# Retrieval layer of a hybrid decoder: splits of the tiles that run ahead moved to GpSimd, one-hot rows moved to VectorE, SyncE's order changed

## The chip, the cores and the metric

One core of one Trainium2 chip runs the whole program. The metric is the device time of one execution in microseconds (us); of several executions the median is given.

## The reference

The program is one inference step of a two-layer decoder for 512 prompt tokens and 32 sample tokens. Each layer has a mixer (attention with a gated recurrence in layer 0, a convolution module in layer 1) and then a retrieval over 128 x 128 experts, which is what the change touches:

```python
q = (xb @ w_q).reshape(blk, PEER_HEADS, 2, PEER_DKH)
sc = jnp.einsum('nhpd,hpkd->nhpk', q, sub_keys)
sv, si = lax.top_k(sc, PEER_TOPK)
cand = sv[:, :, 0, :, None] + sv[:, :, 1, None, :]
cidx = si[:, :, 0, :, None] * N_KEYS + si[:, :, 1, None, :]
fv, fi = lax.top_k(cand, PEER_TOPK)
eidx = jnp.take_along_axis(cidx, fi, axis=-1)
gate = jax.nn.softmax(fv, axis=-1)
act = gelu(einsum('nd,nhed->nhe', xb, u_tab[eidx]))
y = einsum('nhe,nhed->nd', gate * act, v_tab[eidx])
```

Every token has 8 heads with 16 chosen experts each. An expert number is a pair of keys (first key, second key), each from 0 to 127.

## The kernel before, in words

For 384 of the tokens (three blocks of 128, `DENSE`) the kernel gathers nothing. It multiplies all tokens with all experts in tiles of 128 experts: 128 tiles of the table U ("units") and 128 of the table V ("values") in each layer, with a gate matrix between them that is zero where a token did not choose an expert. The other two blocks (`LONE`) gather their rows by indirect DMAs on GpSimd.

A tile's way: SyncE loads it (512 KB) into one of four `raw` buffers. ScalarE copies it to the ring in a rounded format (`hi`, L1005). The difference of the two, the low part, is the **split** (`low` on VectorE, L1572; `lo` on GpSimd, L1902, which is used for the tiles of the projections only). Then TensorE takes it: `units` (L850) makes 24 matmuls of 384 columns, `values` (L862) 18 of 512. Matmuls of a tile wait for `lo_ready`, and for units also for the Gelu (L1091) of the tile two before, since there are two PSUM halves.

While the gate matrix is not there, 48 units tiles run ahead (`AHEAD`); their Gelu results go through three buffers `ga` (`ASLOT`) to DRAM by SyncE (`write_units`) and come back later. In this time the ring has four slots only, so `hi` of tile i + 3 waits for the matmuls of tile i - 1. The stage goes thus, in each layer:

- **Front**: 26 tiles (`FRONT`). VectorE makes the choices of three token blocks (`select`, 15 parts, two LONE blocks and the first DENSE one) with the splits between the parts (`SEL_QUANTA`).
- **Gates with tiles**: 32 groups of eight tokens (16 for each of blocks 0 and 1), a tile after each second group (`MID` = 16 tiles). For a group VectorE and ScalarE make two sets of eight one-hot rows: `oh1`, first key times gate weight, eight `tensor_scalar` on VectorE (L1560); `oh2`, second key, three on VectorE (L1556) and five on ScalarE (`Abs` into `dist`, L1052, then one `Relu`, L1057). TensorE multiplies them (`gate_group`, L833), ScalarE stages the result (`stage_group`, L1123 and L1129). Between the groups VectorE makes the next block's choice, one part after each group, and after each second group the split of one tile.
- **Gates alone**: the last 16 groups, with no tile between them, two one-hots of eight on ScalarE.
- **Six tiles** (42 to 47), then two more units tiles and the first tile of values.

After every eighth group SyncE writes the staged 4 MB to DRAM in two DMAs (`write_gates`); the staging buffer is single, so ScalarE's first copy of the next eight waits for them. TensorE may be two groups ahead of ScalarE's copies and VectorE two ahead of TensorE. `choice` (L819) transposes a block's choices on TensorE; ScalarE copies them (`slT`, L1137) and the block's one-hots can begin.

Every engine works through its own list in the order in which it is written; SyncE's list (`experts`, L450) goes by tiles: at step i it loads tile i + 7 (after the split of tile i + 3, which had the same raw buffer), then writes the unit of tile i - 2. GpSimd's list has the gathers (`gather_rows`) next; they wait until all groups are staged.

Of the kernel before, what the change touches and what calls it, by code (L numbers as in the profile page):

```python
# [21 lines left out]
F32 = mybir.dt.float32  # L22
F32R = mybir.dt.float32r
U32 = mybir.dt.uint32
ALU = mybir.AluOpType
# [3 lines left out]
P = 128  # L29
# [18 lines left out]
ACT_OH_BUSY, ACT_OH_FREE = 5, 2  # L48
# [21 lines left out]
AHEAD, FRONT, MID = 48, 26, 16  # L70
# [31 lines left out]
def ready_by(i):  # L102
# [4 lines left out]
SEL_QUANTA = [(0, (0,)), (0, (1, 2, 3, 4, 5)), (0, (6, 7, 8, 9, 10, 11, 12, 13, 14))] + [  # L107
    (i, parts) for i in (1, 2) for parts in ((0,), (1, 2), (3, 4, 5), (6, 7), (8,), (9, 10), (11,), (12, 13), (14,))]
EXP_AFTER = {[m for m, (s, parts) in enumerate(SEL_QUANTA) if s == i and 4 in parts][0]: i for i in range(3)}

# [78 lines left out]
def build(nc, xT, stream, utab, vtab, params, consts, mconsts, reset, keysT, kcacheT, vcache, kvcache_n, state_h, convT,  # L189
          yT, kwin_p, vwin_p, hs_p, cb_p, kwin_s, vwin_s, hs_s, cb_s):  # L190
    ctx = ExitStack()
    with ctx:
# [84 lines left out]
        with ExitStack() as z:  # L277
            with ExitStack() as zz:
                hf_peer = sb("hf_peer", [P, KC, NT], F32, zz)
            with ExitStack() as zz:  # L280
                oh2 = sb("oh2", [P, 2, 8, P], F32, zz)
                oh1 = sb("oh1", [P, 2, 8, P], F32, zz)
            sb("ohpad", [P, KC * NT], F32, z)
            with ExitStack() as zz:
                keys = sb("keys", [P, 16, P], F32, zz)
                qh = sb("qh", [P, 2, NT], F32, zz)
                sc2 = sb("sc2", [P, 4, P], F32, zz)
            with ExitStack() as zz:
                ga = sb("ga", [P, ASLOT, ND], F32, zz)
                pick = sb("pick", [P, 3, 16, NCAND], F32, zz)  # L290
            sb("keypad", [P, 16 * P + 2 * NT + 5 * P], F32, z)
            sv = sb("sv", [P, NTILE, 16, 16], F32, z)
            si = sb("si", [P, NTILE, 16, 16], U32, z)
            sif = sb("sif", [P, 16, 16], F32, z)
            cand = sb("cand", [P, 8, NCAND], F32, z)
            cand2 = sb("cand2", [P, 8, NCAND], F32, z)
            cidx = sb("cidx", [P, 8, NCAND], F32, z)
            fv = sb("fv", [P, 8, 16], F32, z)
            fi = sb("fi", [P, 8, 16], U32, z)
            pos = sb("pos", [P, 8, 16], F32, z)  # L300
            eidx = sb("eidx", [P, 8, 16], F32, z)
            r16 = sb("r16", [P, 8, 16], F32, z)
            r8 = sb("r8", [P, 2, 8], F32, z)
            sel = sb("sel", [P, 3, 8, 16], F32, z)
            slT = sb("slT", [P, 2, 3, P], F32, z)
            dist = sb("dist", [P, max(ACT_OH_BUSY, ACT_OH_FREE), P], F32, z)
# [102 lines left out]
        def _(sp):  # L409
# [40 lines left out]
            def experts(l):  # L450
                for i in range(7):
                    load_expert(l, i)
                for i in range(N_EXP):
# [4 lines left out]
                    if i >= AHEAD - 2 and tile_at(i + 4)[1]:  # L458
                        load_gate(l, V_SEQ[tile_at(i + 4)[2]])
                    if i + 7 < N_EXP:  # L460
                        load_expert(l, i + 7)
                    if 2 <= i < AHEAD + 2:
                        write_units(l, i - 2)
                    h, r = divmod(i - FRONT - 3, 4)
                    if r == 0 and 0 <= h < 3:
                        write_gates(l, h)
                    if i == FRONT + MID - 1:
                        for h in range(3, 6):
                            write_gates(l, h)
# [65 lines left out]
        s_oh = sem("dve_onehots_ready")  # L535
        s_oha = sem("act_onehots_ready")
# [53 lines left out]
        def _(pe):  # L590
# [246 lines left out]
            def experts(l):  # L837
# [33 lines left out]
                for m in range(MID):  # L871
                    gate_group(l, 2 * m)
                    gate_group(l, 2 * m + 1)
                    if m % 8 == 7:
                        choice(l, m // 8 + 1)
                    units(FRONT + m)
                for g in range(2 * MID, ND // 8):
                    gate_group(l, g)
                for i in range(FRONT + MID, AHEAD):
                    units(i)  # L880
# [115 lines left out]
        def _(act):  # L996
# [48 lines left out]
            def onehots(l, n, q):  # L1045

                e = (ND // 8) * l + n * 16 + q
                k = ACT_OH_BUSY if n + 1 < NDB else ACT_OH_FREE
                if e:
                    act.wait_ge(s_oha, e)  # L1050
                for i in range(k):
                    ch.done(A.activation(dist[:, i, :], iota, ACT.Abs, scale=-1.0,  # L1052
                                         bias=slT[:, n % 2, 1, 8 * q + i:8 * q + i + 1]))
                ch.sync()
                if n * 16 + q >= 2:
                    act.wait_ge(s_gm, e - 1)
                A.activation(oh2[:, e % 2, 0:k, :], dist[:, 0:k, :], ACT.Relu, scale=-1.0,  # L1057
                             bias=ones[:, 0:1]).then_inc(s_oha, 1)

# [21 lines left out]
            def experts(l):  # L1081
# [19 lines left out]
                def tile_step(i):  # L1101
# [5 lines left out]
                    if i < FRONT and i - 1 in EXP_AFTER:  # L1107
                        select_exp(l, EXP_AFTER[i - 1])
# [26 lines left out]
                for n in DENSE:  # L1135
# [3 lines left out]
                    act.wait_ge(s_slT, NDB * l + n + 1)  # L1139
                    onehots(l, n, 0)  # L1140
                    for q in range(16):
                        if q + 1 < 16:
                            onehots(l, n, q + 1)
# [3 lines left out]
                        if q % 2 and n + 1 < NDB:  # L1147
                            tile_step(FRONT + 8 * n + q // 2)
                for i in range(FRONT + MID, N_EXP):
# [230 lines left out]
        def _(dve):  # L1380
# [164 lines left out]
            def onehots(l, n, q):  # L1545
# [6 lines left out]
                k = ACT_OH_BUSY if n + 1 < NDB else ACT_OH_FREE  # L1552
                if n * 16 + q >= 2:
                    dve.wait_ge(s_gm, e - 1)
                for j in range(k, 8):
                    ch.done(V.tensor_scalar(oh2[:, e % 2, j, :], iota, slT[:, n % 2, 1, 8 * q + j:8 * q + j + 1],  # L1556
                                            None, ALU.is_equal))
# [9 lines left out]
            def experts(l):  # L1567
# [47 lines left out]
                def tile_step(i):  # L1615
                    for j in range(ready_by(i - 1) if i else 3, ready_by(i)):
                        low(t0 + j)

                dve.wait_ge(s_lo, t0 + 3)
                for i in range(FRONT):  # L1620
                    if i < len(SEL_QUANTA):
                        s, parts = SEL_QUANTA[i]
                        for part in parts:
                            select(l, s, part)
                    tile_step(i)
                for n in DENSE:
                    for q in range(16):
                        onehots(l, n, q)
                        if n + 1 < NDB:
                            if q >= 1:  # L1630
                                select(l, 3 + n, q - 1)
                            if q % 2:
                                tile_step(FRONT + 8 * n + q // 2)
                n_row = 0
                for i in range(FRONT + MID, N_EXP):
                    tile_step(i)
# [262 lines left out]
        def _(pool):  # L1899
# [9 lines left out]

            def gather_rows(l):  # L1910
# [40 lines left out]
            lo_run(T_WQ[0], T_WQ[0] + N_WQ + 3)  # L1951
            gather_rows(0)
# [10 lines left out]
            lo_run(T_WQ[1], T_WQ[1] + N_WQ + 3)  # L1963
            gather_rows(1)
# [118 lines left out]
```

## Time and profile before

| | us |
|---|---|
| median of 3 executions | 3833.21 |
| lowest, highest | 3825.51, 3833.39 |
| the profiled execution | 3821.67 |
| its span, first to last instruction | 3819.9 |
| TensorE busy | 3301.6 (86%) |
| VectorE busy | 2786.7 (73%) |
| ScalarE busy | 1460.5 (38%) |
| GpSimd busy | 1190.3 (31%) |

All durations below come from the profiled execution, whose 3821.67 us are 1.77 us more than its span. The stage of the change comes twice: at 637.6 to 1128.3 us (layer 0) and at 2460.6 to 2953.6 us (layer 1). A row of the profile reads: line of the code, engine, operation, tile written<-tiles read, shapes, count, busy time, mean time of one in ns, idle time before it and what ended it. PE is TensorE, DVE VectorE, ACT ScalarE, POOL GpSimd, SP SyncE. A row of the timeline has start and length in us; several instructions in a row of one line are merged ("x8"), and their starts lie closer than their lengths, since one instruction's end overlaps the next one's start.

### The profile page before, as it was taken

What the parts mean: (1) busy time and instruction counts of PE and PEld (TensorE: products, weight loads), DVE (VectorE), ACT (ScalarE), POOL (GpSimd) and SP (SyncE); (2) the same over time, 40 slices, a digit from 0 to 9 for tenths busy, and PEclk for the clock granted to TensorE, in tenths of its full rate; (3) what the DMA queues carried; (4) which work ended last, traced back from release to release, by engine and by line L of the source; (5) the groups of instructions that cost most, each with busy time, mean ns of one, the idle gap of its engine ahead of it and who ended that gap; (6) DMA issues with size and microseconds to landing.
All of it is one profiled execution on the core that took longest, in us unless ns stands there. A gap on an engine that the chain in (4) does not pass through costs nothing. (4 is left out here: it accounts for less than half of the span.)

```text
span 3819.9 us, 50346 instructions
## 1 busy us (share of the span) xinstructions
PE 3301.6 (86%) x18573; PEld 3004.1 (79%) x18573; DVE 2786.7 (73%) x6082; ACT 1460.5 (38%) x2215; POOL 1190.3 (31%) x766
## 2 busy tenths in 40 slices
PE   6877899956679999999978879996667999999998
PEld 5767788955578888888867658986656888888887
DVE  4426457866658888888866964796665888888887
ACT  3433222466643333333323222236655333333332
POOL 2210321000025555555542112100001555555554
PEclk9988699988889999999998989998878999999999
DMA  3110312523269999999961141252235999999997
GB/s 116 47 48 1 96 63 77 167 90 112 97 250 381 363 361 363 366 361 361 361 234 61 39 54 52 67 167 98 90 126 205 380 365 364 369 359 363 360 364 264
DMA packets 424997, 807.91 MB, mean 212 GB/s; under 512 B 233953, under 2 KB 259105, under 8 KB 421281
## 3 DMA queue, kind: packets, MB, share of 16 engines
q1 hardware_dynamic: 318960, 454.23, 35.7%
q0 software_dynamic: 94560, 344.45, 24.3%
q10 hardware_dynamic: 11232, 6.01, 1.2%
q8 instruction: 148, 2.42, 0.3%
q14 instruction: 97, 0.79, 0.1%
HBM read 729.52 MB, written 76.08 MB: 211 GB/s over the span
## 5 line engine op out<-in xcount | busy, mean ns | idle before, releaser
L850 PE MATMUL bank<-hh,ring 128*128 128x384 f32 x4096 | 1096.2, 341 | 45.9 <-ACT ga L1091 36.7
L1572 DVE TENSOR_TENSOR ring<-raw,ring 128x1024 fp32r<-128x1024 f32 x506 | 618.3, 1223 | 458.7 <-ACT ring L1005 458.2
L1921 POOL DMA_INDIRECT rows<-in_utab,gidx x320 | 452.4, 1414 | 1335.9 <-ACT stage L1129 891.0
L862 PE MATMUL bank<-ring,wh 128*128 128x512 f32 x3072 | 828.3, 391 | 0.0
L850 PEld LDWEIGHTS bank<-hh,ring 128*128 128x128 f32 x4096 | 750.8, 190 | 58.5 <-issue 41.2
L1005 ACT ACTIVATE ring<-raw 128x1024 fp32r<-128x1024 f32 x598 | 622.1, 1053 | 193.9 <-PE bank L850 87.1
L850 PE MATMUL bank<-hl,ring 128*128 128x384 f32 x2048 | 691.0, 337 | 0.0
L862 PEld LDWEIGHTS bank<-ring,wh 128*128 128x128 f32 x3072 | 574.4, 188 | 111.3 <-issue 0.2
L1921 POOL DMA_INDIRECT rows<-in_vtab,gidx x320 | 491.1, 1535 | 368.4 <-DVE acc L1612 316.0
L611 PE MATMUL bank<-hh,ring 128*128 128x272 f32 x2752 | 493.8, 299 | 74.8 <-DVE hl L1397 43.5
L1091 ACT ACTIVATE ga<-bank 128x384 f32<-128x384 f32 x256 | 125.4, 490 | 1100.3 <-PE bank L850 997.3
L611 PEld LDWEIGHTS bank<-hh,ring 128*128 128x128 f32 x2752 | 408.9, 196 | 88.6 <-issue 51.6
L833 PE MATMUL bank<-oh 128*128 128x128 f32 x1536 | 258.8, 340 | 248.1 <-DVE oh L1560 214.7
L862 PE MATMUL bank<-ring,wl 128*128 128x512 f32 x1536 | 473.1, 389 | 0.0
L833 PEld LDWEIGHTS bank<-oh 128*128 128x128 f32 x1536 | 240.6, 247 | 269.7 <-DVE oh L1560 235.7
L1902 POOL TENSOR_TENSOR ring<-raw,ring 128x1024 fp32r<-128x1024 f32 x92 | 223.6, 2438 | 677.0 <-ACT ring L1005 674.4
L1612 DVE SCALAR_TENSOR_TENSOR acc<-rows,wv,acc 128x1024 f32<-128x1024 f32 x316 | 404.5, 1280 | 12.3 <-DVE acc L1612 0.5
L850 PEld LDWEIGHTS bank<-hl,ring 128*128 128x128 f32 x2048 | 389.5, 190 | 6.1
L1604 DVE CUSTOM_DVE_ANT_0 rows<-rows,htok 128x1024 f32<-128x1024 f32 x320 | 381.8, 1219 | 0.7 <-DMA rows<-in_utab,gidx 0.7
L862 PEld LDWEIGHTS bank<-ring,wl 128*128 128x128 f32 x1536 | 288.3, 188 | 64.1
L611 PE MATMUL bank<-hl,ring 128*128 128x272 f32 x1376 | 293.1, 295 | 0.0
L611 PEld LDWEIGHTS bank<-hl,ring 128*128 128x128 f32 x1376 | 226.1, 196 | 0.0
(299 smaller groups left out, 3166.6 us busy)
## 6 DMA issues: line engine op xcount, KB each, us to landing
raw<-in_stream SPq DMA_DIRECT2D x342, 512.0 KB, 4.4
raw<-in_vtab SPq DMA_DIRECT2D x256, 512.0 KB, 7.7
gate_matrix<-stage SPq DMA_DIRECT2D x24, 2048.0 KB, 10.2
gt<-gate_matrix SPq DMA_DIRECT2D x256, 192.0 KB, 9.4
units_ahead<-ga SPq DMA_DIRECT2D x96, 192.0 KB, 4.1
gv<-units_ahead SPq DMA_DIRECT2D x96, 192.0 KB, 8.8
rows<-in_utab,gidx POOLq DMA_INDIRECT x320, 7.9
rows<-in_vtab,gidx POOLq DMA_INDIRECT x320, 8.0
```

Of the source, the lines that this page charges most:

```text
L611: m = T.matmul(PA[t % 2][:, a, 0:HALF], w[:, ring_slot(t), k * P:(k + 1) * P], h[:, k, a * HALF:(a + 1) * HALF], start=(k == 0 and i == 0) ...
L833: m = T.matmul(PA[e % 2][:, i // 4, (i % 4) * P:(i % 4 + 1) * P], oh2[:, e % 2, i, :], oh1[:, e % 2, i, :], start=True, stop=True)
L850: m = T.matmul(PB[1][:, (e + 1) % 2, 0:ND], w[:, ring_slot(t), k * P:(k + 1) * P], h[:, k, 0:ND], start=(k == 0 and i == 0), stop=(k == KC ...
L862: m = T.matmul(psum[c][:, a, :], w[:, v_n % WSLOT, c * P:(c + 1) * P], v[:, ring_slot(t), 512 * a:512 * a + 512], start=(v_n == 0 and i == ...
L1005: A.activation(ring_hi[:, ring_slot(t), :], raw[b][:], ACT.Copy).then_inc(s_hi, 1)
L1091: A.activation(ga[:, e % ASLOT, :], PB[1][:, (e + 1) % 2, 0:ND], ACT.Gelu).then_inc(s_ga, 1)
L1572: V.tensor_tensor(ring_lo[:, ring_slot(t), :], raw[raw_buffer(t)][:], ring_hi[:, ring_slot(t), :].bitcast(F32), ALU.subtract).then_inc(s_l ...
L1604: V.tensor_tensor_reduce(out=rows[:, slot, :], in0=rows[:, slot, :], in1=htok[b][:, :], scale=1.0, scalar=0.0, op0=ALU.mult, op1=ALU.add, ...
L1612: V.scalar_tensor_tensor(out=acc[b][:, :], in0=rows[:, slot, :], scalar=wv[b][:, j:j + 1], in1=acc[b][:, :], op0=ALU.mult, op1=ALU.add).th ...
L1902: nc.gpsimd.tensor_tensor(ring_lo[:, slot, :], raw[buf][:], ring_hi[:, slot, :].bitcast(F32), ALU.subtract).then_inc(s_lo, 1)
L1921: nc.gpsimd.indirect_dma_start(out=rows[:, g % ROW_SLOTS, :], out_offset=None, in_=vtab if is_v else utab, in_offset=bass.IndirectOffsetOn ...
```

## The change

GpSimd makes the splits of tiles 3 to 47 in a list of its own (`ahead`), before the gathers. VectorE makes all of `oh2` with one `tensor_tensor` over 8 x 128 elements a group, and ScalarE makes no one-hots. VectorE makes the three choices of the front without splits between them. 24 tiles run in the front; in the gates, tiles come after groups 1, 3, 5 (one each) and 7 (two) of each eight for the first 32 groups, two come after group 39, and the last two after group 47. ScalarE's exponentials of the three choices (`select_exp`) come at tile steps 3, 8 and 19. SyncE writes unit i - 1 before it loads tile i + 7, and each `write_gates` stands at the step of the tiles that follow its eighth group.

```diff
-AHEAD, FRONT, MID = 48, 26, 16
+AHEAD, FRONT = 48, 24
...
+TILES_AFTER = [0] * (ND // 8)
+for _g in range(ND // 8):
+    if _g < 32:
+        TILES_AFTER[_g] = {1: 1, 3: 1, 5: 1, 7: 2}.get(_g % 8, 0)
+TILES_AFTER[39] = 2
+TILES_BEFORE = [FRONT + sum(TILES_AFTER[:_g]) for _g in range(ND // 8)]
+EXP_BEFORE = {3: 0, 8: 1, 19: 2}
...
+                    if 1 <= i <= AHEAD:
+                        write_units(l, i - 1)
                     if i + 7 < N_EXP:
                         load_expert(l, i + 7)
-                    if 2 <= i < AHEAD + 2:
-                        write_units(l, i - 2)
-                    h, r = divmod(i - FRONT - 3, 4)
-                    if r == 0 and 0 <= h < 3:
-                        write_gates(l, h)
-                    if i == FRONT + MID - 1:
-                        for h in range(3, 6):
+                    for h in range(ND // 64):
+                        if i == TILES_BEFORE[8 * h + 7] - 1:
                             write_gates(l, h)
...
-                for m in range(MID):
-                    gate_group(l, 2 * m)
-                    gate_group(l, 2 * m + 1)
-                    if m % 8 == 7:
-                        choice(l, m // 8 + 1)
-                    units(FRONT + m)
-                for g in range(2 * MID, ND // 8):
+                i = FRONT
+                for g in range(ND // 8):
                     gate_group(l, g)
-                for i in range(FRONT + MID, AHEAD):
+                    for m in range(TILES_AFTER[g]):
+                        units(i)
+                        i += 1
+                        if g % 16 == 15 and m == 0:
+                            choice(l, g // 16 + 1)
+                for i in range(i, AHEAD):
                     units(i)
...
-                    onehots(l, n, 0)
                     for q in range(16):
-                        if q + 1 < 16:
-                            onehots(l, n, q + 1)
                         stage_group(n, q)
                         if q == 6 and n + 1 < NDB:
                             select_exp(l, 3 + n)
-                        if q % 2 and n + 1 < NDB:
-                            tile_step(FRONT + 8 * n + q // 2)
-                for i in range(FRONT + MID, N_EXP):
+                        for m in range(TILES_AFTER[16 * n + q]):
+                            tile_step(TILES_BEFORE[16 * n + q] + m)
+                for i in range(TILES_BEFORE[-1], N_EXP):
                     tile_step(i)
...
-                for j in range(k, 8):
-                    ch.done(V.tensor_scalar(oh2[:, e % 2, j, :], iota, slT[:, n % 2, 1, 8 * q + j:8 * q + j + 1],
-                                            None, ALU.is_equal))
+                V.tensor_tensor(oh2[:, e % 2, :, :], iota.unsqueeze(1).to_broadcast([P, 8, P]),
+                                slT[:, n % 2, 1, 8 * q:8 * q + 8].unsqueeze(2).to_broadcast([P, 8, P]),
+                                ALU.is_equal).then_inc(s_oha, 1)
...
-                dve.wait_ge(s_lo, t0 + 3)
-                for i in range(FRONT):
-                    if i < len(SEL_QUANTA):
-                        s, parts = SEL_QUANTA[i]
-                        for part in parts:
-                            select(l, s, part)
-                    tile_step(i)
+                for i in range(3):
+                    for part in range(NPART):
+                        select(l, i, part)
                 for n in DENSE:
                     for q in range(16):
                         onehots(l, n, q)
-                        if n + 1 < NDB:
-                            if q >= 1:
-                                select(l, 3 + n, q - 1)
-                            if q % 2:
-                                tile_step(FRONT + 8 * n + q // 2)
+                        if n + 1 < NDB and q >= 1:
+                            select(l, 3 + n, q - 1)
+                dve.wait_ge(s_lo, t0 + AHEAD)
                 n_row = 0
-                for i in range(FRONT + MID, N_EXP):
-                    tile_step(i)
+                for i in range(AHEAD - 3, N_EXP):
+                    for j in range(ready_by(i - 1), ready_by(i)):
+                        low(t0 + j)
...
+            def ahead(l):
+
+                def tile_step(i):
+                    for j in range(ready_by(i - 1) if i else 3, min(AHEAD, ready_by(i))):
+                        lo(T_EXP[l] + j, ring_slot(T_EXP[l] + j), raw_buffer(T_EXP[l] + j))
+
+                for i in range(FRONT):
+                    tile_step(i)
+                for g in range(ND // 8):
+                    for m in range(TILES_AFTER[g]):
+                        tile_step(TILES_BEFORE[g] + m)
+
...
             lo_run(T_WQ[0], T_WQ[0] + N_WQ + 3)
+            ahead(0)
             gather_rows(0)
```

## Rows read from the trace of the kernel before

**Rows 1.** Windows by stage, layer 0: length, busy time by engine, clock, DMA share, GB/s.
```profile
637.60:761.10 123.50, 114.57 (x627) 111.12 (x627) 111.62 (x327) 51.24 (x71) 4.62 (x2) 0.97 0.54 159
761.10:1016.80 255.70, 157.20 (x902) 148.78 (x902) 166.61 (x575) 159.24 (x267) 0.00 (x0) 0.83 0.28 96
1016.80:1083.30 66.50, 37.51 (x257) 35.27 (x258) 48.67 (x210) 42.12 (x59) 0.00 (x0) 0.85 0.31 131
1083.30:1128.30 45.00, 35.02 (x193) 34.73 (x192) 14.77 (x18) 14.79 (x19) 8.96 (x7) 0.89 0.83 289
```

**Rows 2.** Waits, 761.1 to 1083.3 us: total us, times, longest.
```profile
PE bank L833 <- DVE oh L1560: 110.1, 39, 13.4
DVE ring L1572 <- ACT ring L1005: 88.0, 16, 13.1
DVE oh L1556 <- PE bank L833: 15.8, 3, 8.4
```

**Rows 3.** Timeline of VectorE in the gates with tiles.
```profile
784.21 1.23 DVE L1572 TENSOR_TENSOR ring<-raw,ring 128x1024 fp32r<-128x1024 f32 x1 [3.75 <-ACT ring L1005]
785.35 0.67 DVE L1556 TENSOR_SCALAR oh<-con,slT 128x128 f32<-128x128 f32 x3
785.94 2.14 DVE L1560 TENSOR_SCALAR oh<-con,slT 128x128 f32<-128x128 f32 x8
```

**Rows 4.** VectorE by line, 644.95 to 741.2 us (the front's three choices).
```profile
L1572 DVE TENSOR_TENSOR ring<-raw,ring 128x1024 fp32r<-128x1024 f32 x21 | 25.6, 1217 | 0.0
L1516 DVE TENSOR_TENSOR pick<-pick,cidx 128x2400 f32<-128x2400 f32 (+1 forms) x7 | 16.1, 2301 | 0.2
L1507 DVE TENSOR_TENSOR pick<-pos,con 128x2400 f32<-128x2400 f32 (+1 forms) x7 | 16.1, 2295 | 0.0
```

**Rows 5.** Waits of the front, 637.6 to 761.1 us.
```profile
ACT ga L1091 <- DMA units_ahead<-ga: 36.2, 16, 5.5
```

**Rows 6.** GpSimd and VectorE by line, 2050 to 2160 us (convolution, layer 1).
```profile
L1902 POOL TENSOR_TENSOR ring<-raw,ring 128x1024 fp32r<-128x1024 f32 x12 | 32.3, 2713 | 69.6 <-ACT ring L1005 69.6
...
L1873 DVE SCALAR_TENSOR_TENSOR cv<-up,par,cv 128x512 f32<-128x512 f32 x87 | 69.9, 803 | 0.0
L1873 DVE SCALAR_TENSOR_TENSOR cv<-us,par,cv 128x32 f32<-128x32 f32 x86 | 35.6, 414 | 0.0
```

**Rows 7.** Timeline of VectorE there, beside splits by GpSimd.
```profile
2058.02 2.37 DVE L1871 TENSOR_SCALAR cv<-us,par 128x32 f32<-128x32 f32 x1
...
2060.76 0.29 DVE L1871 TENSOR_SCALAR cv<-us,par 128x32 f32<-128x32 f32 x1
...
2093.82 0.24 DVE L1873 SCALAR_TENSOR_TENSOR cv<-us,par,cv 128x32 f32<-128x32 f32 x1
2093.98 0.75 DVE L1873 SCALAR_TENSOR_TENSOR cv<-up,par,cv 128x512 f32<-128x512 f32 x1
2094.64 2.41 DVE L1873 SCALAR_TENSOR_TENSOR cv<-us,par,cv 128x32 f32<-128x32 f32 x1
```

**Rows 8.** GpSimd and VectorE by line, 2340 to 2422 us (retrieval, layer 1).
```profile
L1902 POOL TENSOR_TENSOR ring<-raw,ring 128x1024 fp32r<-128x1024 f32 x12 | 28.8, 2400 | 91.7 <-ACT ring L1005 91.7
...
L1454 DVE FIND_INDEX8 si<-sv,sc 128x8 uint32<-128x128 f32 x40 | 10.7, 285 | 0.0
```

**Rows 9.** The chain that ended last, layer 1's gates alone: start, length.
```profile
2841.03 12.96 DMA gate_matrix<-stage
2873.05 2.07 PE bank L833 x16
2875.14 1.95 ACT stage L1129
2877.47 10.80 DMA gate_matrix<-stage
2909.38 4.18 PE bank L850 x24
```

**Rows 10.** DMA issues (the page): KB each, median us to landing.
```profile
gt<-gate_matrix SPq DMA_DIRECT2D x256, 192.0 KB, 9.4
```

More of the change, by code:

```diff
@@ L47 @@
 DENSE, LONE = (0, 1, 2), (4, 3)
-ACT_OH_BUSY, ACT_OH_FREE = 5, 2
 NPART = 15
@@ L104, in ready_by @@
     return min(N_EXP, i + (4 if i < AHEAD + 4 else 5))
-SEL_QUANTA = [(0, (0,)), (0, (1, 2, 3, 4, 5)), (0, (6, 7, 8, 9, 10, 11, 12, 13, 14))] + [
-    (i, parts) for i in (1, 2) for parts in ((0,), (1, 2), (3, 4, 5), (6, 7), (8,), (9, 10), (11,), (12, 13), (14,))]
-EXP_AFTER = {[m for m, (s, parts) in enumerate(SEL_QUANTA) if s == i and 4 in parts][0]: i for i in range(3)}
+TILES_AFTER = [0] * (ND // 8)
[5 more added lines that the diff above has]
+EXP_BEFORE = {3: 0, 8: 1, 19: 2}
 ROW_SLOTS = 5
@@ L305, in build @@
             slT = sb("slT", [P, 2, 3, P], F32, z)
-            dist = sb("dist", [P, max(ACT_OH_BUSY, ACT_OH_FREE), P], F32, z)
         with ExitStack() as z:
@@ L534, in build @@
         s_slT = sem("selection_T_ready")
-        s_oh = sem("dve_onehots_ready")
-        s_oha = sem("act_onehots_ready")
+        s_oh = sem("key1_onehots_ready")
+        s_oha = sem("key2_onehots_ready")
         s_ht = sem("lone_tokens_transposed")
@@ L1043, in attn_out @@
                     .then_inc(s_oe, 1)
[L1045 to L1058, printed above, removed]
             def retrieval(l):
@@ L1106, in tile_step @@
                         hi(t0 + j)
-                    if i < FRONT and i - 1 in EXP_AFTER:
-                        select_exp(l, EXP_AFTER[i - 1])
+                    if i in EXP_BEFORE:
+                        select_exp(l, EXP_BEFORE[i])
                     if i and not tile_at(i - 1)[1]:
@@ L1138, in experts @@
                                  ACT.Copy).then_inc(s_slT, 1)
-                    act.wait_ge(s_slT, NDB * l + n + 1)
-                    onehots(l, n, 0)
                     for q in range(16):
-                        if q + 1 < 16:
-                            onehots(l, n, q + 1)
                         stage_group(n, q)
@@ L1551, in onehots @@
                         dve.wait_ge(s_ht, 2 * (l + 1))
-                k = ACT_OH_BUSY if n + 1 < NDB else ACT_OH_FREE
                 if n * 16 + q >= 2:
                     dve.wait_ge(s_gm, e - 1)
-                for j in range(k, 8):
-                    ch.done(V.tensor_scalar(oh2[:, e % 2, j, :], iota, slT[:, n % 2, 1, 8 * q + j:8 * q + j + 1],
-                                            None, ALU.is_equal))
+                V.tensor_tensor(oh2[:, e % 2, :, :], iota.unsqueeze(1).to_broadcast([P, 8, P]),
+                                slT[:, n % 2, 1, 8 * q:8 * q + 8].unsqueeze(2).to_broadcast([P, 8, P]),
+                                ALU.is_equal).then_inc(s_oha, 1)
                 for j in range(8):
@@ L1613, in row @@
                                                in1=acc[b][:, :], op0=ALU.mult, op1=ALU.add).then_inc(s_rd, 1)
-                def tile_step(i):
-                    for j in range(ready_by(i - 1) if i else 3, ready_by(i)):
-                        low(t0 + j)
-                dve.wait_ge(s_lo, t0 + 3)
-                for i in range(FRONT):
-                    if i < len(SEL_QUANTA):
-                        s, parts = SEL_QUANTA[i]
-                        for part in parts:
-                            select(l, s, part)
-                    tile_step(i)
+                for i in range(3):
+                    for part in range(NPART):
+                        select(l, i, part)
                 for n in DENSE:
@@ L1963, in _ @@
             lo_run(T_WQ[1], T_WQ[1] + N_WQ + 3)
+            ahead(1)
             gather_rows(1)
```

## The prediction, made before the changed kernel was run

> **What bounds the kernel now.** I read the windows by stage first. Before its values begin (at 1128.3 us in layer 0), a layer spends 490.7 us on tiles that run ahead and on gates; layer 1 spends 493.0 (from 2460.6 to 2953.6). There TensorE is busy for 157.2 of 255.7 us in the gates with tiles and for 37.5 of 66.5 in the gates alone, at a granted clock of 0.83 to 0.85 of 2.4 GHz [rows 1]. So the waits come next. TensorE waits 110.1 us for VectorE's one-hots, but VectorE is not full either (166.6 of 255.7): it waits 88.0 us for ScalarE's copies before the 16 splits [rows 1, 2]. The timeline shows the loop: the split (it had waited 3.75 us) stands ahead of the next one-hots [rows 3]; it waits for a copy, the copy for a ring slot, the slot for a tile on TensorE, and that tile stands behind the groups that wait for one-hots. In the front VectorE has no idle time while it makes the three choices, from 645 to 741 us, with 21 splits among them [rows 4]. So VectorE sets the front's pace and a closed loop through VectorE, TensorE and ScalarE that of the gates. The chain of waits adds the DMA of the staged gates, 10.8 to 13 us for four MB [rows 9].
>
> **What the change costs and gives, per layer.** *A split on GpSimd* takes 2.40 us [rows 8], less than the 4.18 us of a tile (24 matmuls, [rows 9]), and its result is needed three tiles later; so GpSimd keeps up. Its price falls on VectorE. In the convolution twelve splits by GpSimd ran beside VectorE's two-input and scalar operations: one of 32 columns took 2.41 us where its like took 0.24, a `tensor_scalar` 2.37 for 0.29 [rows 7]. Twelve splits made the 86 short ones mean 414 ns and the 87 long ones 803 instead of 240 and 750 [rows 6, 7], that is 15.0 + 4.6 us, and two `tensor_scalar` some 4 more: 24 us, **2.0 us of VectorE a split** when VectorE does nothing else. `FIND_INDEX8`, with one input, keeps its 285 ns beside GpSimd [rows 8]. No row shows a reduction or the choices beside a split. The ends are 0 and 2.4 us a split (GpSimd's whole length); I weigh the 2.0 by the share of VectorE's time in operations like those that were held, and take a reduction as free, since it has one input like `FIND_INDEX8`.
>
> *Front.* 96.25 us hold 21 splits of 1.14 us (784.21 to 785.35 in [rows 3]), so the choices alone are 72 us. The two large two-input groups are 32.2 of them [rows 4]; with the small two-input and scalar ones I estimate 41, a share of 0.57, so 1.2 us a split. While they last GpSimd makes some 23 (one a tile): 645 + 72 + 27 = 744 us. TensorE would end its 23rd tile at 637.6 + 6 (the first one, at the lower clock) + 22 x 4.18 = 736, so it waits for `choice` until 744. Transpose and copy take two more: first one-hots at 746, against 758.4 (0.59 + 2.1 us of one-hots before the first group at 761.1, [rows 1, 3]). **Gain 12.** SyncE's new order takes away the 36.2 us that ScalarE waited for units written late [rows 5]: the write no longer stands behind a load that waits for a split. I cost it at nothing, since the choices cover it; were they shorter, TensorE's 736 would be the next to be late. The load now stands behind the Gelu, but that follows the copy, and the split that the load waits for anyway ends later.
>
> *Gates with tiles.* VectorE's work is 166.6 - 16 x 1.23 = 147 us. One `oh2` of 8 x 128 replaces three that take 0.59 us (785.35 to 785.94): 1024 elements took 1.14 from start to start [rows 3], and repeated operands cost no more by the row, 2295 ns for the 2400 and 1600 elements of L1507 [rows 4]: +0.55 x 32 = 18. Twenty splits at 1.7 (one-hots and two-input parts are 138 of 165 us, 0.84 of the time, by 2.0) are 34. Two hand-overs to the next block, in which `slT` waits behind ScalarE's second tile step, are 5 each. 147 + 18 + 34 + 10 = 209 us against 255.7. **Gain 46.** TensorE's work in it, 32 groups of 2.05 and 20 tiles of 4.18, is 149 us at the full clock, so VectorE is the bound. ScalarE loses its share of the one-hots; it was not last, so that is nothing by itself. The four tiles more than before are TensorE time inside VectorE's. After each eighth group two tiles (8.3) and two groups cover the 13 us write. SyncE waits for that eighth group with one unit write and the loads behind it; seven tiles are loaded by then, so nobody waits.
>
> *Gates alone.* A group costs VectorE 1.14 + 2.05 = 3.2 us as before (six `tensor_scalar` and eight). First group to last: seven groups 22.4, two splits 4; then group 40's copy waits for the write: 2.07 + 1.95 + 11 to 13 after the one-hots of group 39, 1 for the copy, 2.07 for group 42, four sets of one-hots: 32; last group 2. Sum 60.5 against 66.5. **Gain 6.**
>
> *Tail.* Before, 45.0 us with 35 of TensorE work (eight tiles). After: four tiles, 17 us; but the first value's gates come later: copy 2, write 13, `gt` 9.4 [rows 10], product and its two parts 3: 27.5. **Gain 17.** GpSimd's gathers stand behind its splits, but they wait for the last group in any case.
>
> Sum 81 a layer. VectorE's waits for TensorE were 15.8 us [rows 2]; under the new rhythm they lie between nothing and that again, and since two octet ends made most of them I take 3. That is 78 a layer, 156 for both. The profiled execution took 3821.7 us: **3666 us**. It lies 11.5 below the median shown, so a median may come out some 10 above.
>
> **Rivals.** *A, the lock is cheap:* splits fall into operations with one input, or GpSimd waits and VectorE doesn't. Then the front is TensorE's (one-hots at 738, gain 20) and the gates cost 180 instead of 209: 37 more a layer, **3592**. For it: the splits start at the same point of each round. Against it: a one-hot set is 3.2 us of nothing but two-input and scalar operations.
>
> *B, more is lost than the sum has:* full 2.4 a split in the front (choices end at 772, a loss of 16 instead of a gain of 12), 2.4 in the gates (-14), TensorE at the lower clock after its pauses so that VectorE waits 15 instead of 3. Gain 24 to 36 a layer (the second without the lower clock), **3750 to 3774**. The clock of 0.83 [rows 1] speaks for some of this; VectorE's slack of two groups against it.
>
> *C, slower: the splits only change hands.* If VectorE's 88.0 us for copies come back as a wait for TensorE's groups (the loop closes through the one-hots' buffers instead of the ring), then 43 splits cost 2.0 instead of 1.17, which is 36 a layer, and `oh2` 18 more; the tail gives 17 back: 37 lost a layer, **3896**. It decides where a round of two groups and a tile takes TensorE longer than VectorE's 12.6 us; by the rows it takes 8.3, and 16.5 if all of it ran at 1.2 GHz. The Trainium skill's page Perfetto Trace Analysis, section Optimizing Scalar/DVE Operations, warns that moving work between VectorE and GpSimd might not help, as they share a port; by that rule this case would be the likely one. The trace agrees on the sharing (2.41 us for 0.24, [rows 7]), but there VectorE had no wait to win back.
>
> *D, the one-hots don't come faster:* if the repeated operands ran at half rate, `oh2` would take 2.2 us, 51 us more a layer: 3768. The 2295 ns of L1507 speak against it [rows 4].
>
> **Numbers.** Forecast 0.62, A 0.15, B 0.14, C 0.05, D 0.02, other 0.02. The range of 8 in 10 is 3590 to 3755: it takes in A and the near end of B. About 0.2% (8 us) is what a measurement of this kernel can tell from no change; all of A, B, D and the forecast lie beyond that, so faster by more has 0.92, within 0.02, slower 0.06.
>
> **What the changed profile would show.** Right: no wait of VectorE for ScalarE's copies in the gates; VectorE nearly without pauses from the first one-hots to the 32nd group, in about 210 us; some 20 one-hots or picks there with 2 us more than their like, at a GpSimd split; `oh2` at 1.2 us; a pause of TensorE near 740 us for `choice`; the values beginning at about 1050 us instead of 1128. Wrong: VectorE waiting for `gate_tokens_done` in every round (C); the gates with tiles under 190 us (A) or over 230 (B); a pause at each staged write of more than 5 us; values that no longer follow without gaps, since the sum leaves the 851 us behind them as they are.

## The result, and the profile after

The changed kernel took **3673.5 us** (median of 4 executions, 3671.2 to 3675.8); the kernel before, on the same chip, 3829.4 (4 executions). The ratio is 0.9594, 95% interval 0.9577 to 0.9612: 4.1% faster. Forecast were 3666 us, within 3590 to 3755. The profiled execution has a span of 3670.3 us, 149.6 less than before.

| | before | after |
|---|---|---|
| span, us | 3819.9 | 3670.3 |
| TensorE busy, share of the span | 86% | 89% |
| VectorE busy, us | 2786.7 | 2843.0 |
| ScalarE busy, us | 1460.5 | 1284.1 |
| GpSimd busy, us | 1190.3 | 1461.5 |

VectorE is busy for longer than before, although it has lost 90 splits; the time came out of waits. The windows by stage, layer 0 (front, gates with tiles, gates alone, six tiles and what follows until the first value), with the columns of [rows 1]:

```profile
638.10:756.30 118.20, 105.51 (x580) 104.32 (x581) 114.33 (x305) 43.85 (x58) 76.27 (x26) 0.93 0.50 159
756.30:962.80 206.50, 162.17 (x999) 158.21 (x997) 193.51 (x485) 94.89 (x84) 65.03 (x20) 0.91 0.39 144
962.80:1022.40 59.60, 43.32 (x305) 41.25 (x306) 51.33 (x136) 31.84 (x21) 2.57 (x1) 0.94 0.32 115
1022.40:1050.50 28.10, 16.72 (x98) 16.43 (x96) 7.13 (x9) 9.29 (x12) 7.25 (x6) 0.84 0.97 357
```

Against [rows 1] that is 123.5 to 118.2, 255.7 to 206.5, 66.5 to 59.6 and 45.0 to 28.1, in sum 78.3 us; in layer 1 it is 77.1 (492.9 to 415.8). In the gates with tiles VectorE is now busy for 193.5 of 206.5 us. The waits of the gates (756.3 to 1022.4 us) answer to [rows 2]: total us, times, longest.

```profile
POOL ring L1872 <- ACT ring L1004: 183.8, 18, 31.2
...
PE bank L832 <- DVE oh L1539: 53.4, 26, 5.5
...
DVE oh L1534 <- ACT slT L1121: 12.5, 2, 7.6
...
DVE oh L1534 <- PE bank L832: 7.3, 3, 3.8
```

The wait for ScalarE's copies, 88.0 us on VectorE before, is now GpSimd's, where nobody stands behind it. TensorE's wait for one-hots has halved, from 110.1 to 53.4. VectorE itself waits only at the two changes of block (12.5) and three times for TensorE (7.3, all of it in the gates alone).

What the splits cost VectorE stands in two views. First the timeline of GpSimd and VectorE in the gates, with a split that ran from 786.30 to 789.08:

```profile
786.30 2.78 POOL L1872 TENSOR_TENSOR ring<-raw,ring 128x1024 fp32r<-128x1024 f32 x1 [8.69 <-ACT ring L1004]
...
783.44 2.13 DVE L1539 TENSOR_SCALAR oh<-con,slT 128x128 f32<-128x128 f32 x8
785.49 0.22 DVE L1482 CAST pos<-fi 128x128 f32<-128x128 uint32 x1
785.63 1.22 DVE L1534 TENSOR_TENSOR oh<-con,slT 128x1024 f32<-128x1024 f32 x1
786.77 4.20 DVE L1539 TENSOR_SCALAR oh<-con,slT 128x128 f32<-128x128 f32 x8
```

Eight `tensor_scalar` take 2.13 us alone and 4.20 beside the split: 2.07 us for one split. The new `oh2` takes 1.14 from start to start, as forecast. Then the lines of VectorE in the gates with tiles (756.3 to 962.8 us), where the held ones (instructions that took longer because a split of GpSimd ran) raise the means:

```profile
L1539 DVE TENSOR_SCALAR oh<-con,slT 128x128 f32<-128x128 f32 x251 | 87.4, 416 | 0.0
L1534 DVE TENSOR_TENSOR oh<-con,slT 128x1024 f32<-128x1024 f32 x32 | 50.4, 1575 | 12.5 <-ACT slT L1121 12.5
```

Counted one by one, ten of the first were held (20.6 us over their 0.33) and eight of the second (11.7 over their 1.21). That is 32.3 us for 20 splits, 1.6 each. In layer 1, 13 and five were held, 34.8 us.

### The profile page after: what moved, and what is told of

The parts are those of the page before. It is cut to its first block and busy times, and to the rows that moved or that the text cites. A ratio compares the mean times of both kernels' runs of the same rounds, so it can differ in the third digit from the quotient of the medians.

```text
span 3670.3 us, 49481 instructions
## 1 busy us (share of the span) xinstructions
PE 3262.9 (89%) x18573; PEld 2976.5 (81%) x18573; DVE 2843.0 (77%) x5704; ACT 1284.1 (35%) x1735; POOL 1461.5 (40%) x856
## 5 line engine op out<-in xcount | busy, mean ns | idle before, releaser
L1872 POOL TENSOR_TENSOR ring<-raw,ring 128x1024 fp32r<-128x1024 f32 x182 | 496.9, 2737 | 1110.2 <-ACT ring L1004 1107.3
L849 PEld LDWEIGHTS bank<-hh,ring 128*128 128x128 f32 x4096 | 752.8, 191 | 27.9 <-POOL ring L1872 14.6
L1551 DVE TENSOR_TENSOR ring<-raw,ring 128x1024 fp32r<-128x1024 f32 x416 | 508.1, 1222 | 205.7 <-ACT ring L1004 205.5
L849 PEld LDWEIGHTS bank<-hl,ring 128*128 128x128 f32 x2048 | 390.6, 191 | 6.1
L861 PEld LDWEIGHTS bank<-ring,wl 128*128 128x128 f32 x1536 | 289.3, 188 | 64.4
L832 PE MATMUL bank<-oh 128*128 128x128 f32 x1536 | 220.6, 305 | 120.2 <-DVE oh L1539 111.6
L832 PEld LDWEIGHTS bank<-oh 128*128 128x128 f32 x1536 | 207.6, 216 | 132.8 <-DVE oh L1539 123.9
L1539 DVE TENSOR_SCALAR oh<-con,slT 128x128 f32<-128x128 f32 x768 | 256.7, 403 | 0.0
```

The lines of the kernel that those rows point to most:

```text
L832: m = T.matmul(PA[e % 2][:, i // 4, (i % 4) * P:(i % 4 + 1) * P], oh2[:, e % 2, i, :], oh1[:, e % 2, i, :], start=True, stop=True)
L849: m = T.matmul(PB[1][:, (e + 1) % 2, 0:ND], w[:, ring_slot(t), k * P:(k + 1) * P], h[:, k, 0:ND], start=(k == 0 and i == 0), stop=(k == KC ...
L861: m = T.matmul(psum[c][:, a, :], w[:, v_n % WSLOT, c * P:(c + 1) * P], v[:, ring_slot(t), 512 * a:512 * a + 512], start=(v_n == 0 and i == ...
L1539: m = V.tensor_scalar(oh1[:, e % 2, j, :], iota, slT[:, n % 2, 0, c:c + 1], slT[:, n % 2, 2, c:c + 1], ALU.is_equal, ALU.mult)
L1551: V.tensor_tensor(ring_lo[:, ring_slot(t), :], raw[raw_buffer(t)][:], ring_hi[:, ring_slot(t), :].bitcast(F32), ALU.subtract).then_inc(s_l ...
L1872: nc.gpsimd.tensor_tensor(ring_lo[:, slot, :], raw[buf][:], ring_hi[:, slot, :].bitcast(F32), ALU.subtract).then_inc(s_lo, 1)
```

## The experiments

All ran beside the kernel before (3825.05 us for the first four, 3825.55 for the others; medians of 7 executions each). The times are medians of 4 executions. The stages of layer 0 in us, cut as above:

| | time | ratio, interval | front | gates with tiles | gates alone | tail | sum |
|---|---|---|---|---|---|---|---|
| before | | | 123.5 | 255.7 | 66.5 | 45.0 | 490.7 |
| after | 3673.5 | 0.9594, 0.9577 to 0.9612 | 118.2 | 206.5 | 59.6 | 28.1 | 412.4 |
| 1 splits back | 3744.6 | 0.9787, 0.9771 to 0.9804 | 111.3 | 252.9 | 58.5 | 27.9 | 450.7 |
| 2 one-hots shared | 3647.3 | 0.9535, 0.9519 to 0.9551 | 117.8 | 196.5 | 60.2 | 28.0 | 402.6 |
| 3 old order on SyncE | 3671.0 | 0.9598, 0.9582 to 0.9614 | 119.1 | 206.6 | 59.6 | 31.3 | 416.6 |
| 4 short splits | 3582.0 | 0.9367, 0.9351 to 0.9383 | 105.2 | 178.0 | 59.2 | 28.1 | 370.6 |
| 5 only the splits | 3716.3 | 0.9711, 0.9691 to 0.9731 | 124.8 | 206.7 | 66.7 | 41.5 | 439.7 |
| 6 tiles moved | 3646.8 | 0.9530, 0.9509 to 0.9550 | 120.0 | 193.2 | 58.8 | 30.4 | 402.4 |
| 7 front on VectorE | 3636.4 | 0.9502, 0.9481 to 0.9523 | 110.8 | 197.6 | 59.9 | 28.3 | 396.6 |
| 8 both | 3638.5 | 0.9512, 0.9489 to 0.9536 | 110.8 | 199.5 | 59.4 | 30.5 | 400.1 |

**1. The splits back on VectorE**, between the parts of the choices as before, with the steps of `select_exp` that belong to that (`EXP_BEFORE`); all else as in the changed kernel:

```diff
-                for i in range(3):
-                    for part in range(NPART):
-                        select(l, i, part)
+                for i in range(FRONT):
+                    ...
+                    tile_step(i)
...
-                dve.wait_ge(s_lo, t0 + AHEAD)
+                        for m in range(TILES_AFTER[16 * n + q]):
+                            tile_step(TILES_BEFORE[16 * n + q] + m)
...
-            ahead(0)
```

> The changed kernel with the splits of the tiles that run ahead back on VectorE, in its list at the same tile steps; everything else as changed. My theory (the gain comes from opening the loop through the splits): VectorE waits some 90 to 110 us a layer for ScalarE's copies again, the gates with tiles take 260 to 285 us instead of 206, the front's first group comes some 5 us earlier; in all 3750 to 3810 us. Rival (the gain comes from where the tiles stand and from SyncE's order, GpSimd's splits only cost VectorE time): at most 3690 us.

3744.6 us: 5 under the expected band, and far from the rival's 3690. The gates with tiles are shorter than the 260 us expected, and the waits less than the 90. Two lines of VectorE in the gates with tiles (754.7 to 1007.6 us):

```profile
L1536 DVE TENSOR_TENSOR oh<-con,slT 128x1024 f32<-128x1024 f32 x33 | 40.1, 1216 | 0.0
L1553 DVE TENSOR_TENSOR ring<-raw,ring 128x1024 fp32r<-128x1024 f32 x20 | 24.5, 1226 | 64.4 <-ACT ring L1006 64.4
```

No one-hot is held (mean 1216 ns), and the splits cost 24.5 us of work, less than the 32.3 that GpSimd's take from VectorE. But 64.4 us of waiting for ScalarE's copies are back ahead of them, and the stage takes 252.9 us. The other parts of the change gain 80 us without the splits: front 12, gates alone 8, tail 17 a layer, and only 3 in the gates with tiles, which take four tiles more. Of the 12, 8.4 are the two tiles that the front has lost (4.18 each, [rows 9]).

**2. One-hots of the second key shared with ScalarE again** (five of eight, two in the last block), as before the change:

```diff
+                        if q + 1 < 16:
+                            onehots(l, n, q + 1)
...
-                V.tensor_tensor(oh2[:, e % 2, :, :], ...
+                for j in range(ACT_OH_BUSY if n + 1 < NDB else ACT_OH_FREE, 8):
+                    ch.done(V.tensor_scalar(oh2[:, e % 2, j, :], iota, ...
```

> The changed kernel with five (in the last block two) of the eight second-key one-hots of a group back on ScalarE, as before the change; splits stay on GpSimd. My theory (VectorE is the bound of the gates with tiles, ScalarE has time to spare): 0.55 us a group less on VectorE, the gates with tiles 17 us a layer shorter, 3630 to 3650 us, faster than the changed kernel's 3673. Rival (taking ScalarE out of the one-hots was part of the gain, since its copies and staging come late behind them): 3680 to 3730 us.

3647.3 us, 26 less than the changed kernel (23 by the ratios): moving these rows to VectorE was a loss, hidden in the gain of the rest. The gates with tiles take 196.5 instead of 206.5 (layer 1: 193.8 instead of 210.9). The window and three waits (758.8 to 955.4 us):

```profile
758.80:955.40 196.60, 162.28 (x1001) 158.37 (x999) 164.85 (x547) 163.21 (x270) 52.80 (x20) 0.90 0.41 150
```

```profile
DVE oh L1556 <- PE bank L834: 18.3, 5, 7.4
...
DVE oh L1556 <- ACT slT L1138: 13.0, 2, 6.5
...
PE bank L834 <- DVE oh L1560: 11.7, 7, 2.9
```

VectorE's busy time falls by 28.7 us, but the stage only by 10: it is no longer VectorE alone that sets the pace, since VectorE now waits 18.3 us for TensorE, and ScalarE is as busy as VectorE.

**3. The old order on SyncE** (unit i - 2 after the load instead of i - 1 ahead of it):

```diff
-                    if 1 <= i <= AHEAD:
-                        write_units(l, i - 1)
                     if i + 7 < N_EXP:
                         load_expert(l, i + 7)
+                    if 2 <= i < AHEAD + 2:
+                        write_units(l, i - 2)
```

> The changed kernel with SyncE's old order of the unit writes (unit i - 2 after the load of tile i + 7). My theory (the choices cover it): ScalarE waits some 30 us a layer in the front for written units again, TensorE stops for choice a little less, 3668 to 3680 us. Rival (the order is a part of the gain): the front's tiles take 4.6 us each again, 8 us a layer, 3685 to 3700 us.

3671.0 us: no difference that could be measured, and in the band, though the 30 us of waits that were expected did not come back. One wait of its front (636.5 to 755.6 us) answers to [rows 5]:

```profile
ACT ga L1075 <- DMA units_ahead<-ga: 2.5, 4, 1.2
```

The 36.2 us that ScalarE waited for late unit writes are gone with the old order too. Four kernels make the table complete: old order with splits on VectorE 36.2 (before), old order with GpSimd's splits 2.5 (here) and 2.1 (run 5), new order with splits on VectorE no such wait (runs 1 and 7). Either cure is enough against these waits. The tail is 3.2 us longer here (4.0 in layer 1: 31.4 for 27.4): TensorE pauses in it for a Gelu that waits for a unit's write (12.5 us), one tile ahead of the first value. Of that 2.3 us come back behind it, where the values take 851.1 us instead of 853.4.

**4. Short splits.** GpSimd's split covers 64 of 1024 columns; the low part of the other 960 is left out for these tiles.

```diff
-                        lo(T_EXP[l] + j, ring_slot(T_EXP[l] + j), raw_buffer(T_EXP[l] + j))
+                        nc.gpsimd.tensor_tensor(ring_lo[:, ring_slot(t), 0:64], raw[raw_buffer(t)][:, 0:64],
+                                                ring_hi[:, ring_slot(t), 0:64].bitcast(F32),
+                                                ALU.subtract).then_inc(s_lo, 1)
```

> The changed kernel in which GpSimd's split of tiles 3 to 47 covers 64 of the 1024 columns only (the low part of the other 960 columns is left out), so that each holds VectorE up for some 0.3 us instead of 2.4. It prices the lock. My theory (1.2 us a split in the choices, 1.7 in the gates): TensorE's pause for choice of 11.6 us goes, the gates with tiles lose 20 x 1.5 = 30 us, the gates alone 4; 45 a layer, 3570 to 3600 us. Rival (the lock is cheap, since the splits fall beside operations that are not held): 3640 to 3670 us.

3582.0 us. The same number of splits, waits and semaphores, only shorter (0.87 us each in the gates), takes 91 us off: 41.8 in layer 0 and 47.3 in layer 1, of which 13 are in the front, 28.5 and 34.5 in the gates with tiles and almost none later. VectorE's lines in the gates (743.2 to 921.2 us) are back at their own lengths:

```profile
L1539 DVE TENSOR_SCALAR oh<-con,slT 128x128 f32<-128x128 f32 x256 | 68.8, 337 | 0.0
L1534 DVE TENSOR_TENSOR oh<-con,slT 128x1024 f32<-128x1024 f32 x33 | 39.9, 1210 | 12.9 <-ACT slT L1121 10.5 <-PE bank L832 2.4
```

So what GpSimd's splits cost by holding VectorE up is measured, by what comes back without it: nearly all of the 91 us, since TensorE had hardly waited for a split itself (no such wait in the gates of the changed kernel, 0.6 us less of it in the front here). In the front the end that comes next shows, TensorE's tiles, in the timeline of VectorE:

```profile
739.82 1.23 DVE L1534 TENSOR_TENSOR oh<-con,slT 128x1024 f32<-128x1024 f32 x1 [14.89 <-ACT slT L1121]
```

VectorE had its choices ready 14.89 us before.

**5. Only the splits**: the kernel before with GpSimd's splits and nothing else.

```diff
-                    for j in range(ready_by(i - 1) if i else 3, ready_by(i)):
+                    for j in range(max(AHEAD, ready_by(i - 1)) if i else 3, ready_by(i) if i else 3):
...
+            def ahead(l):
+
+                for j in range(3, AHEAD):
+                    lo(T_EXP[l] + j, ring_slot(T_EXP[l] + j), raw_buffer(T_EXP[l] + j))
```

> The kernel before with one edit: GpSimd makes the splits of tiles 3 to 47, VectorE none of them; tiles, one-hots and the order on SyncE stay as they were. My theory (the splits on VectorE close the loop with ScalarE's copies; opening it is what pays, and the other parts are small): the front about 123 us as before, the gates with tiles 185 to 200 instead of 256 (16 splits at about 2 us on top of 147 us of VectorE's own work), the gates alone 66 and the tail 45 as before; in all 3690 to 3720 us. The rival (the loop stays closed, since ScalarE still makes five of eight one-hots and its copies stand between them, so that the new one-hots and the new places of the tiles were needed too): the gates with tiles over 225 and 3760 us or more.

3716.3 us, in the expected band and far from the rival, yet the gates with tiles took 206.7 us and not 185 to 200. Two waits there (766.7 to 973.4 us) go with the difference:

```profile
ACT stage L1123 <- DMA gate_matrix<-stage: 36.4, 6, 9.3
...
DVE oh L1556 <- PE bank L833: 26.5, 6, 12.0
```

With the old places of the tiles and of the gate writes ScalarE waits 36.4 us for the staged writes (9.8 in all the gates of the changed kernel, the gates alone included), and VectorE 26.5 for groups that wait for it. The splits alone thus take 49 us off the gates with tiles, as much as the whole change does there, and little elsewhere (3.5 in the tail). Run 1 has the rest. By stage the two add up to 40.0 + 51.0 = 91 us in layer 0, against 78.3 for both together: of the 13 that are missing 6 are in the front, where GpSimd's splits cost time once the tiles are fewer, 3 in the gates with tiles, 1 in the gates alone and 4 in the tail.

**6. The tiles moved**: run 2 with 26 tiles in the front, 18 in the gates, none after group 39 and four at the end; GpSimd's list goes on past the last group for them.

```diff
-AHEAD, FRONT = 48, 24
+AHEAD, FRONT = 48, 26
...
-        TILES_AFTER[_g] = {1: 1, 3: 1, 5: 1, 7: 2}.get(_g % 8, 0)
-TILES_AFTER[39] = 2
+        TILES_AFTER[_g] = {1: 1, 3: 1, 5: _g // 8 % 2, 7: 2}.get(_g % 8, 0)
```

> The second run's kernel (one-hots of the second key shared with ScalarE again) with the tiles placed otherwise: 26 instead of 24 ahead of the gates, 18 among the first 32 groups, none after group 39 and four after the last group, where the write of the last gates has to land anyway. If VectorE's one-hots set the pace of the gates, two tiles fewer among them are two held splits (4 us) and the two ahead of the gates cost no more than they do there (up to 8.4); the four at the end cover the write: between 6 us less and 4 us more a layer than the second run's 3647 us, 3635 to 3655, most likely 3635. The rival (TensorE's tile time is what counts wherever it stands) gives the same time as the second run or more: 3650 to 3665.

3646.8 us, the same as run 2: inside the band, but the gain that was held most likely (3635) did not come. Front +2.2, gates with tiles -3.3, gates alone -1.4, tail +2.4 us in layer 0. What two stages gain by a pair of tiles fewer, the two others lose.

**7. The front's splits on VectorE**: run 2, with GpSimd's splits only from the gates on.

```diff
-EXP_BEFORE = {3: 0, 8: 1, 19: 2}
+EXP_BEFORE = {2: 0, 6: 1, 15: 2}
...
-                for i in range(FRONT):
-                    tile_step(i)
```

(the second cut is in `ahead`; VectorE's front is that of run 1)

> The second run's kernel with the splits of the 24 tiles ahead of the gates on VectorE, between the parts of the choices as in the kernel before, and those among the gates on GpSimd. The first run (all splits on VectorE) had the front at 111.3 us a layer where GpSimd's splits have 118: if a held split costs VectorE more than the 1.15 us of making it, as the short split says, this takes 6 to 7 us a layer off the second run: 3632 to 3638. The rival (the first run's front was short only because its tiles came otherwise) gives 3645 to 3650.

3636.4 us, 10.9 less than run 2, as expected, and **the fastest kernel here that computes everything**, 0.9502 of before. In its timeline the end of the choices:

```profile
742.81 0.06 DVE L1546 MEMSET small<- 128x1 f32 x1
...
743.88 0.49 PE L822 MATMUL bank<-con,sel 128*128 128x128 f32 x3
```

They end 103.5 us after the front's start at 639.3, against 110.8 in the changed kernel, and TensorE comes to them 1 us later: both engines end together. The rival, that run 1's front was short only through the places of its tiles, is refuted. Here, where VectorE never waited for ScalarE's copies, a split that it makes itself is cheaper than one that holds it up.

**8. Both**: run 7 without the two tiles after group 39.

```diff
-TILES_AFTER[39] = 2
```

> The third kernel of this set with, besides, no tiles after group 39 and four instead of two left after the last group. The last two splits of the tiles ahead then fall after the one-hots and the write of the last gates is covered by four tiles: 2 to 4 us a layer less than the third kernel, 3625 to 3632. The rival (the last write is on the path, and the tiles in front of it cost nothing): the same as the third kernel or up to 10 us more.

3638.5 us, no difference from run 7: a miss again, as the rival had it. The gates alone gain 0.5 and the tail loses 2.2 in layer 0. The gates with tiles, whose code is the same in both kernels, differ by 1.9 us in layer 0 and by 2.9 the other way in layer 1 (195.1 and 192.2), so a difference of 2 or 3 us in that stage is not to be read.

## Why the prediction was right, and where it was not

**The loop in the gates** was read rightly. It forecast 209 us and 3 of stalls; the two layers took 206.5 and 210.9. Its terms: held splits 34 (measured 32.3 and 34.8), hand-overs to the next block 10 (12.5 and 14.1), VectorE's waits for TensorE 3 (none in this stage, 7.3 in the gates alone of layer 0), `oh2` 0.55 more a group (1.14 from start to start). Run 1 shows that the splits carry this gain, run 5 that they alone give it.

**Gates alone** were put at 60.5 and took 59.6; **the tail** at 27.5 and took 28.1. Runs 1 and 5 show that the splits did not make these two. With the one-hots or the order of the unit writes put back (runs 2 and 3) the gates alone stay at 60.2 and 59.6 and the tail at 28.0 and 31.3, which leaves the new places of the tiles and of the gate writes, which no run puts back alone.

**The front** is the term that was mis-sized: a gain of 12 was forecast, 5.3 came (layer 1: 6.6). Three things were wrong there.

First, "VectorE sets the front's pace" was a misreading. VectorE was without idle time until 741 us, but nobody waited for it then. The sum did not use this, since it set the new first one-hots against the measured 758.4, but it hid what did set the pace. In the kernel before, VectorE ends its choices and TensorE comes to them nearly 15 us later; the timeline of both engines there:

```profile
741.11 0.06 DVE L1543 MEMSET small<- 128x1 f32 x1
...
755.90 0.49 PE L819 MATMUL bank<-con,sel 128*128 128x128 f32 x3
...
758.39 0.67 DVE L1556 TENSOR_SCALAR oh<-con,slT 128x128 f32<-128x128 f32 x3
```

TensorE came last by its 26 tiles and by its waits in that front (637.6 to 761.1 us) for Gelus; 5 of these 8.4 us are three waits for a Gelu that had itself waited for a late unit write [rows 5]:

```profile
PE bank L850 <- ACT ga L1091: 8.4, 8, 3.1
```

Second, the price. The choices were to end at 744 us at 1.2 a split; the timeline after, of VectorE and TensorE, shows 749:

```profile
748.91 0.06 DVE L1523 MEMSET small<- 128x1 f32 x1
...
749.03 0.90 PE L818 MATMUL bank<-con,sel 128*128 128x128 f32 x3 [11.04 <-DVE small L1523]
...
750.49 1.22 DVE L1534 TENSOR_TENSOR oh<-con,slT 128x1024 f32<-128x1024 f32 x1 [1.52 <-ACT slT L1121]
...
756.27 3.73 PE L832 MATMUL bank<-oh 128*128 128x128 f32 x32
```

The choices ran for 103.5 us (645.4 to 749.0), 31 more than the 72 alone, which is 1.3 for each of GpSimd's 24 splits in that time (2.0 x 0.57 gave 1.14, which the prediction took as 1.2, for 23). The lines of VectorE in the front (645 to 750 us), against [rows 4]:

```profile
L1496 DVE TENSOR_TENSOR pick<-pick,cidx 128x2400 f32<-128x2400 f32 (+1 forms) x7 | 28.6, 4085 | 0.2
L1487 DVE TENSOR_TENSOR pick<-pos,con 128x2400 f32<-128x2400 f32 (+1 forms) x7 | 21.7, 3093 | 0.2
L1503 DVE TENSOR_REDUCE eidx<-pick 128x48 f32<-128x2400 f32 (+1 forms) x7 | 16.1, 2296 | 0.2
...
L1445 DVE CAST sif<-si 128x256 f32<-128x256 uint32 (+1 forms) x3 | 2.9, 981 | 0.1
```

The two large groups grew by 12.5 and 5.6 us, and the reduction not at all, against this line of the kernel before (644.95 to 741.2 us):

```profile
L1523 DVE TENSOR_REDUCE eidx<-pick 128x48 f32<-128x2400 f32 (+1 forms) x7 | 16.0, 2290 | 0.0
```

So that assumption held, and the share of held operations as a measure was nearly right. But the row of `FIND_INDEX8` in [rows 8] could not carry it: none of the 40 instructions of L1454 ran beside a split. All 40 of the other `FIND_INDEX8` in that window (2340 to 2422 us) did, and they took no longer:

```profile
L1441 DVE FIND_INDEX8 si<-sv,bank 128x8 uint32<-128x128 f32 x40 | 10.9, 290 | 0.0
```

Against run 7, where VectorE makes the splits, the choices end 7 us later.

Third, behind the choice TensorE has the front's last tile to do before the first group. The prediction counted to the first one-hots, and those came 8 us earlier (758.4 to 750.5). But after its pause of 11.04 us TensorE took 6.7 us for that tile (749.58 to 756.27) instead of 4.18, at a granted clock of 0.50 (1.2 GHz) until 754.9 and of 1.00 from then, and the first group waited for it, although its one-hots were ready at 753.7. In the whole front the granted clock fell from 0.97 [rows 1] to 0.93.

**SyncE's order** was costed at nothing, and beside GpSimd's splits the time shows nothing (run 3): those take away the 36.2 us as well. The reason given, that the choices cover these waits, is one for the changed kernel, where the choices end last. In the kernel before TensorE came last and lost some 5 us to the late writes. What the new order alone would be worth there no run shows.

**Behind the stage** the sum left the values as they were; they take 853.4 instead of 851.1 us in layer 0. The 2.3 us are the first value's: TensorE had been idle for 11.4 us when it began, and its 18 matmuls take 6.4 us (from 1050.45), at a granted clock of 0.53 until 1055.5, instead of 4.1 (from 1128.31 before, at 1.00).

The errors nearly cancel in the sum, in layer 0: front -6.7, gates with tiles and stalls +6.2 (49.2 against 46 less 3), gates alone +0.9, tail -0.1, behind -2.3, so 76 where 78 were forecast. The profiled execution was forecast at 3666 and took 3672.1: that the two lie so close is luck, since the front's error met one of the other sign; that the gates came out is not.

**The rivals.** Run 4 is what A supposed, held operations for next to nothing, and gives 3582.0 where A had 3592: so A was a right price for a condition that the kernel does not meet. Of B's loss in the front a part happened: the choices ended 5 us after the forecast's 744, where B had 28, and TensorE ran at the lower clock behind its pause. C is refuted: VectorE's 88.0 us came back as 7.3 for TensorE. The Trainium skill's page Perfetto Trace Analysis, section Optimizing Scalar/DVE Operations, warned that such a move might not help. Its reason is seen here (32.3 us of VectorE for work that had taken 24.5 in run 1), and in the front it decides (run 7); in the gates the move gave 46 us all the same (252.9 in run 1 to 206.5), because it took a wait away and not work. D is refuted by 1.14 us a group.

## What to carry to other kernels

A split that was moved to GpSimd cost VectorE more than it saved (1.6 us in the gates and 1.3 in the front for 1.14). The move paid where VectorE had waited for the split's input with other work queued behind, and did not where VectorE had no such wait (run 7). An engine without idle time isn't the bound until somebody waits for its result: look at who comes to the hand-over last. And a change that gains as a whole can hold a part that loses: undoing one part at a time found 26 us in one and 11 in another.

## What the runs showed of the hardware

How many inputs an operation has does not tell whether it is held up: a conversion with one input is, though a reduction with one is not. In the front's timeline a conversion beside a split takes 2.37 us, against 0.29 for one four times as large with no split beside it; the reduction (L1503 above) keeps its length:

```profile
645.30 2.41 POOL L1872 TENSOR_TENSOR ring<-raw,ring 128x1024 fp32r<-128x1024 f32 x1 [0.27 <-ACT ring L1004]
...
645.39 2.37 DVE L1445 CAST sif<-si 128x64 f32<-128x64 uint32 x1
...
661.13 0.29 DVE L1445 CAST sif<-si 128x256 f32<-128x256 uint32 x1
```

GpSimd is held up in turn: a split takes 2.40 us at the front's start, three in a row 11.53 beside VectorE's large picks, and 3.26 us in the mean among the one-hots (65.0 us for 20):

```profile
642.63 2.40 POOL L1872 TENSOR_TENSOR ring<-raw,ring 128x1024 fp32r<-128x1024 f32 x1
...
684.32 11.53 POOL L1872 TENSOR_TENSOR ring<-raw,ring 128x1024 fp32r<-128x1024 f32 x3 [1.01 <-ACT ring L1004]
```
